# In the RWKV recurrence, the next chunk's exponentials leave the centring's level: three go one level later, the two long ones to the scaling's level

## What is computed

```
def _wkv7(r, w_log, k, v, a, b):
    decay = jnp.exp(-jnp.exp(w_log.astype(f32)))
    ...
    def step(state, inp):
        r_t, w_t, k_t, v_t, a_t, b_t = inp
        sa = jnp.einsum('bhvk,bhk->bhv', state, a_t)
        state = (state * w_t[:, :, None, :] + sa[..., None] * b_t[:, :, None, :]
                 + v_t[..., None] * k_t[:, :, None, :])
        return state, jnp.einsum('bhvk,bhk->bhv', state, r_t)
```

## Time and profile before

| | us |
|---|---|
| three runs: lowest, median, highest | 1454.08, 1456.61, 1458.19 |
| profiled execution: from first to last instruction (span) | 1449.7 |
| median less the span | 6.9 |
| PE busy | 1305.1 (90%) |
| DVE busy | 748.0 (52%) |
| ACT busy | 347.5 (24%) |
| POOL busy | 244.6 (17%) |

### The profile page before, as it was taken

One profiled execution on the slowest core, in us unless ns is written; L12 is line 12 of the kernel. 1 busy time (PEld: TensorE's weight loads), 2 busy tenths in 40 slices (PEclk: granted clock), 3 DMA queues, 4 the chain that ended last, 5 costly groups with the idle time before them and its releaser, 6 DMA issues.

```text
span 1449.7 us, 22238 instructions
## 1 busy us (share of the span) xinstructions
PE 1305.1 (90%) x8266; PEld 854.6 (59%) x8266; DVE 748.0 (52%) x1474; ACT 347.5 (24%) x786; POOL 244.6 (17%) x262
## 2 busy tenths in 40 slices
PE   2989999998999999799999699999999996999990
PEld 2578867656444444585843577777786454444440
DVE  5677573754222233878336567777764234222224
ACT  4000146002211110101058434433432012111111
POOL 0000047000110002100002423333333000010003
PEclk9899899897999999899999799999999997999995
DMA  9677555654799996311110000000003123899985
GB/s 367 197 262 288 188 203 204 225 181 163 236 343 358 361 364 232 131 70 47 59 58 1 31 2 2 20 2 2 2 2 117 58 77 126 290 352 351 336 292 217
DMA packets 128851, 247.25 MB, mean 171 GB/s; under 512 B 8208, under 2 KB 78048, under 8 KB 128768
## 3 DMA queue, kind: packets, MB, share of 16 engines
q1 hardware_dynamic: 116496, 203.04, 40.7%
q0 software_dynamic: 7056, 25.69, 4.9%
q10 hardware_dynamic: 5216, 17.36, 3.0%
HBM read 218.28 MB, written 27.79 MB: 170 GB/s over the span
## 4 chain that ended last, share of the span: by engine, by line
PE 56%; DMA 24%; DVE 11%; issue 4%; ACT 2%; SPq 1%; POOL 1%; POOLq 0%; DVEq 0%; ACTq 0%
DMA WR<-in_moe_w 21%; PE PS L2047 13%; PE PS L2013 8%; PE PS L1968 5%; PE PS L2185 3%; PE PS L2329 2%; PE PS L2378 2%; PE PS L1941 2%; PE PS L2266 2%; DMA arena<-in_ada_w 2%; PE PS L2360 2%; DVE arena L1314 2%; PE PS L2117 1%; PE PS L2445 1%; SPq L726 1%
## 5 line engine op out<-in xcount | busy, mean ns | idle before, releaser
L2185 PE MATMUL PS<-WR,arena 128*128 (+1 forms) x528 | 233.5, 595 | 11.6 <-ACT arena L1130 6.3
L2185 PEld LDWEIGHTS PS<-WR,arena 128*128 128x128 f32 x528 | 97.7, 190 | 125.4 <-issue 121.5
L1570 DVE TENSOR_TENSOR arena<-arena,PS 128x256 f32<-128x256 f32 x33 | 13.9, 421 | 207.2 <-ACT arena L1143 178.8
L2047 PE MATMUL PS<-WR,arena 128*128 128x256 f32 x480 | 111.7, 393 | 4.3 <-DVE arena L1692 4.2
L2013 PE MATMUL PS<-WR,arena 128*128 128x512 f32 x256 | 112.3, 595 | 0.0
L2204 PE MATMUL PS<-W,arena 128*128 x248 | 111.9, 592 | 0.0
L2047 PEld LDWEIGHTS PS<-WR,arena 128*128 128x128 f32 x480 | 94.2, 198 | 20.3 <-DVE arena L1692 3.4
L1314 DVE SCALAR_TENSOR_TENSOR arena<-arena,cact 128x1024 f32<-128x1024 f32 x77 | 99.6, 1294 | 12.4 <-DMA arena<-in_ada_w 6.5
L1968 PE MATMUL PS<-arena,WR 128*128 128x512 f32 x192 | 86.0, 604 | 1.1 <-DVE arena L1401 1.1
L2013 PEld LDWEIGHTS PS<-WR,arena 128*128 128x128 f32 x256 | 48.1, 191 | 56.2 <-issue 56.2
L864 POOL TENSOR_TENSOR LO<-GB,tmp 128x256 f32<-128x256 f32 x80 | 68.0, 870 | 71.2 <-DVE GB L1766 56.9
(11 more groups left out here) (375 smaller groups left out, 2129.0 us busy)
## 6 DMA issues: line engine op xcount, KB each, us to landing
WR<-in_moe_w SPq DMA_DIRECT2D x66, 1024.0 KB
arena<-in_ada_w SPq DMA_DIRECT2D x82, 512.0 KB, 4.6
W<-in_moe_w SPq DMA_DIRECT2D x33, 1024.0 KB
expert_rows<-arena ACTq DMA_DIRECT2D x31, 512.0 KB, 7.5
WR<-in_rwkv_w_rkv SPq DMA_DIRECT2D x6, 2048.0 KB, 8.5
WR<-in_mix_w_in SPq DMA_DIRECT2D x5, 2048.0 KB, 10.0
WR<-in_mix_w_out SPq DMA_DIRECT2D x2, 2048.0 KB, 7.9
expert_rows<-arena SPq DMA_DIRECT2D x1, 4096.0 KB, 14.6
```

The lines of the kernel that those rows point to most:

```text
L2047: last = mm(out[:, n * 256:n * 256 + 256], left, right, start=(c == 0), stop=(c == 3))
L2185: last = mm(PS[:, 2, :], XgT[:, c, :], WR[:, slot, c, :].rearrange("p s f -> p (s f)"), start=(c == 0), stop=(c == KC - 1))
```

## The change

One line of `scan_steps` makes the queue `ahead`. Before, its second entry was centre and exponents together, its third exponents2, its fourth scale. Now the second is centre alone, the third exponents, the fourth exponents2 and scale.

```
-        ahead = [[(k, c + 1) for k in ks] for ks in (("cumulate",), ("centre", "exponents"), ("exponents2",), ("scale",),
+        ahead = [[(k, c + 1) for k in ks] for ks in (("cumulate",), ("centre",), ("exponents",), ("exponents2", "scale"),
                                                      ("place",)) if c + 1 < KC]
```

## The result

| | before | after |
|---|---|---|
| median of 7 runs each (us) | 1458.19 | 1446.0 |
| lowest to highest | 1453.63 to 1460.54 | 1443.31 to 1448.2 |
| span of the profiled execution | 1449.7 | 1441.5 |

The ratio of the runs is 0.9938, with a 95% interval of 0.9918 to 0.9958: 0.6% faster, between 6 and 12 us. The medians in the table lie 12.2 us apart, just beyond the far end of that; the profiled executions differ by 8.2 us. The forecast was 1448.0, in a range of 1445.0 to 1453.5, from 8.6 us less. The changed kernel's profiled run took 1443.31, 1.8 us more than its span.

The account below looks back on a forecast made before the run. It took PE, 56% of the chain, to bound the kernel, standing for ACT's late copies of X. 5.7 us (six turns) plus 2.9 (turn 0) gave 8.6 less: 1456.61 - 8.6 = 1448.0, range 1445.0 to 1453.5.

Parts of the forecast that it names:

- Level 2, 0.95 a turn, 5.7 in all: Turns 1 to 6: with the three exponentials behind X's copy, T comes 0.95 us earlier a turn, 5.7 us in all.
- the two bounds: T's gain at level 2 a turn: at least the recorded idle, 0.89 us, at most 0.95 from turn 7; 0.95 taken.
- Level 3 at no cost: The three exponentials, 0.73 us, ahead of level 3's copy of X cost nothing; the copy starts at about 899.65.
- Level 4 at no cost, 0.59 in hand: The two long exponentials, 1.05 us, ahead of level 4's copy of X cost nothing, with 0.05 + 0.54 us in hand.
- the 0.05 for ACT's idle: At level 4 the 1.05 us of exponentials fit into ACT's 1.10 us of idle time with 0.05 to spare.
- DVE at no cost: DVE's scaling has 0.88 us in hand, and level 2's transposes are 0.2 us late at most; neither costs anything.
- Turn 0, 2.9: In turn 0 T of level 3 starts near 827.7 instead of 830.58, 2.9 us earlier; about 3.0 to T of level 4.
- Two of the signs: Line 2378's idle for line 1214 falls from 8.1 to under 1 us; T of level 4 shows none for it.
- The clock: Turn 0's slow stretch at 829 to 832 goes, sum 8.6 us; rival: it stays, 7.0 us, 1449.6, chance 0.14.
- The tail: Rival: seven of layer 1's 14 expert loads come out slower, losing 6.5 us and leaving 2.1, 1454.5; chance 0.12.
- the 6.9 us around the span: The median of the runs, 1456.61, lies 6.9 us above the profiled span of 1449.7.
- The slower side: Rival: level 4's copy of X waits behind all five exponentials; 3.4 us slower, 1460.0, chance 0.06.

Follow-up runs that it names:

- long_two_only: The kernel before with only the two long exponentials moved to the scaling's entry, the three left with the centring; period 36.68 us, ratio to before 0.9998.
- five_after_level2: The kernel before with all five exponentials in the queue's third entry (level 2) and the scaling alone in the fourth; period 35.73 us, ratio to before 0.9933.
- early_warm: centring_early with 12 useless products added on PE ahead of R2's second part; period 37.95 us, ratio to before 1.0052.
- pad_09: The changed kernel with nine more small exponentials (128x4) on ACT ahead of line 1196; period 35.89 us, one run.
- five_at_scaling: The kernel before with all five exponentials moved to the scaling's entry, ahead of level 4's copy of X; period 35.76 us, ratio to before 0.9939.
- centring_early: The kernel before with DVE's centring one level earlier, right behind the running sum, and ACT's order unchanged; period 39.35 us, ratio to before 1.0104.

## Why the prediction was right

**What bounds.** ACT has 2% of the chain, and yet the edit of ACT's order was worth 0.6%, since PE stood for it. Long_two_only and five_after_level2 split the change: with the three exponentials in their old place the period is before's to 0.01 us, with them moved it is the change's to 0.01 us. Early_warm, where ACT's wait is taken away by another means, has T of level 2 at the same 1.67 us behind X.

**Level 2, 0.95 a turn, 5.7 in all.** Measured 36.68 - 35.73 = 0.95, and 5.70 for the six turns. The choice between the two bounds was right: the recorded idle (0.89) was 0.06 short, and turn 7 had the exact figure, because it already was the changed level.

**Level 3 at no cost.** X's copy of level 3 began at 895.73, and T of level 3 had no recorded wait in any of the six turns. The copy started 0.15 us earlier in its turn than forecast: with 3.77 us between the two timelines (895.64 and 891.87) it is 899.50, for 899.65. Five_after_level2 puts a further 1.05 us there at no cost in the six turns, so the cover, Y2 and dS2, was much more than needed.

**Level 4 at no cost, 0.59 in hand.** Right in sign, 0.11 short in size: 0.70 by pad_09. The wrong term is the 0.05 for ACT's idle. In the changed kernel line 1198 starts at 899.41, the copy at 900.09, 0.68 later, where a copy that directly follows such an exponential starts 0.52 later (901.97 to 902.49 in five_at_scaling): so 0.16 was left, not 0.05. I had let the exponentials begin when T's last copy ends, while they begin 0.1 before (line 1196 at 898.88, T's copies from 898.15 to 898.99).

**DVE at no cost.** PE waits for the sum of line 1798 as it did before, 2.3 us in 8 places in both kernels, and for line 1741 not at all.

**Turn 0, 2.9.** From line 2309's starts 2.83. T of level 3 was forecast near 827.7 and came at 827.85. From there to T of level 4 it was 2.92 us for the forecast 3.0. Two of the signs that I had named did not come out so. Line 2378's idle for line 1214 was to fall under 1 us and is 1.3; and T of level 4 shows 0.63 us of idle for line 1214 in turn 0, in all three profiles of the change, which I had called a sign of being wrong. The sum for turn 0 had both in it, T of level 3 behind the centring's end and T of level 4 behind 1.05 us of exponentials; the list of signs left them out. In the six turns there is no such wait. What the sum did not have is T of level 2 waiting for DVE's transposes in this turn: 0.3 us in the change's third profile, 0.8 in its second, 0.7 to 0.8 in five_after_level2, five_at_scaling and the two with small exponentials more, none in the first. That the 2.9 was met to 0.1 us is in part luck. From level 2's X to line 2309 it is 14.98 us in the one profile of before, and 12.12, 12.47 and 12.32 in the three of the change, so 2.5 to 2.9 less; long_two_only, with the three in their old place, took 16.57, for its slow stretch was longer. Counted from level 0's X the table has 3.0 to 3.5, as that X too ran slow (1.97 us) in before and in two of the three, and not in the first (1.16).

**The clock.** The slow stretch went in all three profiles of the change, as forecast with more weight than its rival, and it is there in long_two_only and centring_early, behind gaps of 3.17 and 3.14 us at T of level 2, with products of 1.97 us. Centring_early and early_warm bear out the direction at another place: the gap costs twice, once itself and once in the clock behind it.

**The tail.** The case of the slower loads did not come: the 14 loads of the chain took 154.6 us before and 153.4 after, 7 and 8 of them under 11. The 1.7 us that the profiled execution loses before them are the clock at line 2013, which scatters from profile to profile; of the 1.4 it wins back, 1.2 are in these loads, and nothing ties them to the change. What I called the 6.9 us around the span was mostly something else: the changed kernel's profiled run lies 1.8 us above its span. The runs on record elsewhere show nearly the same distance, 1.7 to 1.9 us in all but two. So before's profiled execution took some 1451.5, an estimate, below all seven of its runs here (lowest 1453.63), and some 5 of the 6.9 us are a fast execution. The forecast set a difference against a median, so this did no harm to the difference. That 1448.0 came within 2.0 us of 1446.0 is in part luck all the same: it was set against a median of 1456.61, and that of the seven runs is 1458.19, 12.2 us above the changed kernel's for the 8.6 that were forecast. The traces account for 8.5 us of this; the rest is within the scatter of the runs.

**The slower side.** It needed level 4's copy 1.49 us late. With five exponentials ahead of it T moved by 0.03 us, and with the long two and nine small ones, the worst that was tried, by 0.16. The forecast gave 0.04 to its being slower by over 0.3%, though its own sum for this case, 3.4 us, is under the 4.4 us of that bound.

## What to carry to other kernels

On an engine that serves another one in order, look at what stands directly ahead of the copy that the busy engine waits for; a wait there for a third engine is paid by both, and moving it behind the copy costs nothing as long as its own reader and the next copy behind it have room. A good price for such a move, exact to 0.01 us here, is a turn of the same loop that lacks the moved step, taken from start to start. And when a wait can be removed either by asking later or by producing earlier, check what the producer does in between: here producing earlier was 1% slower than doing nothing.

## What was not expected of the hardware

A gap of up to 1.77 us on PE in each turn of centring_early cost about 2 us a turn beyond the gap. In turn 2 PE was busy for 1.53 of the 3 us that hold the gap, and the granted clock was 0.60, then 0.50, in the two stretches of 3 us behind them. The gaps of 0.89 us a turn in the kernel before left it at 1.00. In the gap-filled kernel useless products made each turn 1.4 us shorter. And the same stretch need not end the same way: ahead of line 2013, where the profiles have PE busy for 0.7 to 1.1 of 3 us, the clock fell in 7 of 13 and stayed in 6.

A float32 product of a 128x128 by a 128x128 was recorded as two matmuls: 12 of them were 24 records and 2.78 us, so 0.23 us a product, twice the 0.11 that I had planned with.
